# The opening of a two-block network in fp32: identity first, x in two transfers, and two modulation units multiplied without a split

## The chip, the cores and the metric

The kernel runs on one core of a Trainium2 chip. Its time is the device time of one launch in microseconds; the median of the runs is compared. The core has five engines that run instruction streams of their own and meet at semaphores: TensorE (PE, with its weight loads PEld), VectorE (DVE), ScalarE (ACT), GpSimd (POOL) and SyncE (SP), which here only sends transfers.

## What is computed

Two transformer blocks on 256 tokens of width 1024, everything in fp32. Only the beginning of the first block matters here:

```python
mod = jax.nn.silu(c) @ w_ada[l] + b_ada[l]          # c: 1024 numbers, w_ada: 1024 x 6144
sh1, sc1, gt1, sh2, sc2, gt2 = jnp.split(mod[:, None, :], 6, axis=-1)
mod_c = jax.nn.silu(c_ctx) @ w_ada[l] + b_ada[l]
h = modulate(rmsnorm(x, g_norm1[l]), sh1, sc1)      # x: 256 x 1024
hc = modulate(rmsnorm(ctx, g_norm1[l]), shc1, scc1) # ctx: 256 x 1024
cq, ckv, kpe, rq, rk, rv, rg = split_proj(h @ w_in[l])
cq_c, ckv_c, kpe_c, rq_c, rk_c, rv_c, rg_c = split_proj(hc @ w_in[l])
```

The first 2048 columns of mod hold the shift sh1 and the scale sc1, without which no h can be made. What follows (two kinds of attention, retention, feed-forward networks, the second block) is the same before and after.

## The kernel before

All weights stream through six raw buffers of 128 x 1024 numbers. A "unit" is one such load, mostly 512 KB: two row tiles of 128 by 512 columns. Units are numbered in the order in which they are used. u0 to u15 are the modulation (panels ada0 to ada3, four units each, of 512 columns), u16 is the first half of cq, u17 and u18 the first two units of rq, u19 the second half of cq, u20 and u21 the rest of rq, u22 to u25 ckvpe (the latent keys), then rk and so on.

TensorE multiplies in the fast format fp32r, so each unit is split: ScalarE copies the raw unit to `w_hi` (rounded), VectorE subtracts it from the raw one into `w_lo`. There are three pairs of split buffers (NSPLIT = 3). VectorE's subtraction raises `unit_ready` by one; TensorE waits for it, and so does SP before it loads the raw buffer again, six units later. The helper `feed_units(n)` on ScalarE and VectorE issues the splits of all units below n that it has not issued yet; where these calls stand among the other work is an order written out by hand, and it decides what waits behind what.

A modulation unit is four products of 512 columns: `c_parts` holds the high and the low halves of silu(c) and silu(c_ctx) in the stationary side, and each of two row tiles is multiplied by `w_hi` and by `w_lo`. `ada(p)` on ScalarE copies the finished row of 512 numbers of a panel into `modrow`; `ada_spread(p)` on TensorE turns it into columns; `spread(p)` on VectorE adds the bias; `gain_column` makes the gain of the norm. x is normalised (`square`, `variance`, GpSimd's power, `scale_rows` on VectorE for the first 128 tokens and `scale_row` on ScalarE for the others) and turned by TensorE in pairs of column tiles (`turn("x1", ...)`); each pair is then made full with gain and shift (`full`, by VectorE or ScalarE) and written as a high and a low half. cq needs pairs 0 and 1 for its first unit and 2 and 3 for its second; rq's units need pair 0, 1, 2 and 3 in turn.

`keep_busy(o, n)` issues n transposes of the identity that nobody reads; BUSY says how many stand where. `chunk_unit` is a modulation unit followed by three of them. `turn_vectors(g)` turns the small vectors of group g (0: c and c_ctx; 1: gains, biases; 2 and 3: the convolution's) into columns, which VectorE copies in `columns(g)`. `claim` takes a PSUM bank and waits until its last user has freed it; `next_small` goes round the banks 4 to 7, and ckvpe claims all four of them before its first product.

The start: SP sends u0, u1, u2, all of x, u3, u4, u5, then the fourteen vectors of groups 1 to 3, then u6 and so on, each from then on when the unit six before is released. ctx follows u15. The norm's tables k1, the decays and the gains follow u19. ScalarE's own queue sends c, c_ctx and the first block of constants `k0` (identity, selector, ones) before its first instruction.

## Time and profile before

| | us |
|---|---|
| median of 3 runs | 863.7 (862.12 to 865.11) |
| the profiled execution | 862.75 |
| its span, first to last instruction | 860.9 |
| TensorE busy | 833.5 (97%) |
| VectorE busy | 588.4 (68%) |
| ScalarE busy | 469.7 (55%) |
| TensorE idle in the first 60 us | 60 - 47.35 = 12.65 |

Durations come from the profiled execution. A busy TensorE is modelled: the record of a product reaches over the start of the next one, so the cost of a product is read from start to start. L901 and the like are lines of the kernel; names such as raw, w_hi or bank stand without their buffer numbers. `k` as an operand is the identity's block.

### The profile page before, as it was taken

The page shows a single profiled execution, that of the slowest core. Times are in us where ns is not written, and L with a number is a line of the kernel's source. Part 1 is how long each engine was busy: PE and PEld are TensorE (multiplying, and loading weights), DVE is VectorE, ACT ScalarE, POOL GpSimd, SP SyncE. Part 2 cuts the span into 40 slices and gives each one's busy share as a digit, 9 for nine tenths or more (in the row PEclk, how much of TensorE's full clock was granted, in tenths as well). Part 3 has the DMA queues.
Part 4 walks back from the last instruction along what each step waited for, and adds up shares of the span by engine and source line. Part 5 has one row for each costly group of instructions (what it writes and reads, how often), then busy time and mean ns, then how long its engine had stood idle before and what let it go on. Part 6 is the DMA issues. An engine that isn't in the chain of part 4 may idle for free. (4 is left out here: it accounts for less than half of the span.)

```text
span 860.9 us, 12797 instructions
## 1 busy us (share of the span) xinstructions
PE 833.5 (97%) x4917; PEld 719.5 (84%) x4917; DVE 588.4 (68%) x917; ACT 469.7 (55%) x757; POOL 17.8 (2%) x24
## 2 busy tenths in 40 slices
PE   5999999999999999999999999999999999999997
PEld 4788888867899999997889977788977788888785
DVE  4775968797687778887756777577446655555444
ACT  6686355266456666663546584556535644454442
POOL 1001000000000000000000000010000000000000
PEclk9999999999999999999999999999999999999999
DMA  9964464154656655568648543244505565555541
GB/s 329 356 221 125 147 209 147 49 160 161 203 180 210 188 177 183 176 204 310 237 148 295 183 152 123 74 138 156 195 4 170 171 195 178 189 179 189 185 157 49
DMA packets 103507, 152.85 MB, mean 178 GB/s; under 512 B 6506, under 2 KB 55702, under 8 KB 103448
## 3 DMA queue, kind: packets, MB, share of 16 engines
q1 hardware_dynamic: 102136, 149.15, 52.9%
q10 hardware_dynamic: 1312, 2.90, 0.9%
q8 instruction: 39, 0.64, 0.3%
q14 instruction: 20, 0.16, 0.1%
HBM read 150.97 MB, written 1.05 MB: 177 GB/s over the span
## 5 line engine op out<-in xcount | busy, mean ns | idle before, releaser
L2071 DVE TENSOR_TENSOR w_lo<-raw,w_hi 128x1024 fp32r<-128x1024 f32 (+1 forms) x244 | 294.5, 1213 | 163.7 <-ACT w_hi L1510 163.0
L1510 ACT ACTIVATE w_hi<-raw 128x1024 fp32r<-128x1024 f32 (+1 forms) x244 | 254.7, 1050 | 205.1 <-PE bank L737 141.7
L735 PE MATMUL bank<-w_hi,hT_hi 128*128 128x512 f32 (+2 forms) x400 | 156.1, 390 | 2.9 <-DVE w_lo L2071 2.4
L737 PE MATMUL bank<-w_hi,hT_lo 128*128 128x512 f32 (+2 forms) x400 | 153.0, 382 | 0.0
L736 PE MATMUL bank<-w_lo,hT_hi 128*128 128x512 f32 (+2 forms) x400 | 152.7, 382 | 0.0
L839 PE MATMUL bank<-hT_hi,w_hi 128*128 128x256 f32 x512 | 145.1, 283 | 0.0
L840 PE MATMUL bank<-hT_lo,w_hi 128*128 128x256 f32 x512 | 145.0, 283 | 0.0
L841 PE MATMUL bank<-hT_hi,w_lo 128*128 128x256 f32 x512 | 145.0, 283 | 0.0
L839 PEld LDWEIGHTS bank<-hT_hi,w_hi 128*128 128x128 f32 x512 | 98.3, 192 | 0.0
L840 PEld LDWEIGHTS bank<-hT_lo,w_hi 128*128 128x128 f32 x512 | 98.3, 192 | 0.0
L841 PEld LDWEIGHTS bank<-hT_hi,w_lo 128*128 128x128 f32 x512 | 98.3, 192 | 0.0
L735 PEld LDWEIGHTS bank<-w_hi,hT_hi 128*128 128x128 f32 x400 | 75.2, 188 | 19.1 <-DVE w_lo L2071 2.8
L737 PEld LDWEIGHTS bank<-w_hi,hT_lo 128*128 128x128 f32 x400 | 75.2, 188 | 14.8
L736 PEld LDWEIGHTS bank<-w_lo,hT_hi 128*128 128x128 f32 x400 | 75.3, 188 | 13.2
L735 PE MATMUL bank<-w_hi,act_hi 128*128 128x512 f32 x176 | 70.7, 402 | 0.3 <-DVE w_lo L2071 0.3
L737 PE MATMUL bank<-w_hi,act_lo 128*128 128x512 f32 x176 | 69.6, 396 | 0.0
L736 PE MATMUL bank<-w_lo,act_hi 128*128 128x512 f32 x176 | 69.6, 395 | 0.0
L735 PEld LDWEIGHTS bank<-w_hi,act_hi 128*128 128x128 f32 x176 | 33.1, 188 | 9.5 <-issue 1.6
L736 PEld LDWEIGHTS bank<-w_lo,act_hi 128*128 128x128 f32 x176 | 33.1, 188 | 8.1 <-issue 0.5
L737 PEld LDWEIGHTS bank<-w_hi,act_lo 128*128 128x128 f32 x176 | 33.1, 188 | 8.0
L1478 POOL TENSOR_TENSOR rstd<-var,mhalf 128x2 f32<-128x2 f32 (+3 forms) x18 | 15.8, 876 | 838.7 <-DVE var L2728 256.2
L1130 PEld LDWEIGHTS bank<-k,prob 128*128 128x128 f32 x104 | 12.3, 141 | 15.5 <-issue 6.8
(341 smaller groups left out, 1197.5 us busy)
## 6 DMA issues: line engine op xcount, KB each, us to landing
raw<-w_up_dram SPq DMA_DIRECT2D x132, 256.0 KB, 3.1
raw<-w_ada_dram SPq DMA_DIRECT2D x48, 512.0 KB, 4.7
raw<-w_down_dram SPq DMA_DIRECT2D x44, 512.0 KB, 3.4
raw<-w_in_dram SPq DMA_DIRECT2D x40, 512.0 KB, 4.3
raw<-w_gate_dram SPq DMA_DIRECT2D x44, 256.0 KB, 2.8
raw<-w_out_dram SPq DMA_DIRECT2D x16, 512.0 KB, 3.3
raw<-wk_x_dram SPq DMA_DIRECT2D x8, 512.0 KB, 4.5
raw<-wv_x_dram SPq DMA_DIRECT2D x8, 512.0 KB, 3.3
```

The lines of the kernel that those rows point to most:

```text
L735: pe.matmul(o, xh, yh, start=first, stop=False, skip_group_check=skip)
L736: pe.matmul(o, xh, yl, start=False, stop=False, skip_group_check=skip)
L737: return pe.matmul(o, xl, yh, start=False, stop=last, skip_group_check=skip)
L839: pe.matmul(o, hi[:, c:c + P], xh[:, k, :], start=f, stop=False, skip_group_check=True)
L840: pe.matmul(o, hi[:, c:c + P], xl[:, k, :], start=False, stop=False, skip_group_check=True)
L841: ins = pe.matmul(o, lo[:, c:c + P], xh[:, k, :], start=False, stop=last, skip_group_check=True)
L1130: ins = pe.transpose(o[:, j * P:(j + 1) * P], prob_of(i)[:, j * P:(j + 1) * P], ident)
L1478: pool.tensor_tensor(rstd[:, r, c:w], var[:, r, c:w], mhalf[:, c:w], ALU.pow).then_inc(rstd_ready, 1)
L1510: act.activation(unit_view(w_hi[n % NSPLIT], u), unit_view(raw[u % NRAW], u), ACT.Copy).then_inc(w_hi_ready, 1)
L2071: dve.tensor_tensor(unit_view(w_lo[n % NSPLIT], u), unit_view(raw[u % NRAW], u), unit_view(w_hi[n % NSPLIT], u).bitcast(F32), ALU.subtract ...
```

## The change

The identity alone goes first on SP's queue, and the selector and the ones go on ScalarE's. x is sent in two halves, behind u4 and u6, each with a semaphore of its own. The convolution's vectors go behind u19, ctx goes behind u17. ScalarE does one Silu on a scratch column before anything else, and does not split any unit before c_parts is made; VectorE likewise. Twelve filler transposes stand ahead of the first product, while those behind u6 to u10 are gone. Units u14 and u15 are multiplied as they landed, in plain fp32, two products a unit in place of four; nobody splits them, and a tiny copy on VectorE raises `unit_ready` by two for them when TensorE is done. `ready_at` gives the new order of these counts. The spreads and the turns of x move among the units, and the fourth spread goes behind cq's first unit. The convolution's vectors are turned behind rq, and their columns and the lower bound's arithmetic are done behind ctx.

```diff
--- before.py
+++ after.py
@@ -272,7 +272,7 @@
-BUSY = {"score": 8, "ada": 3, "cq": 8, "ffnpre": 14, "gu0": 8}
+BUSY = {"score": 8, "start": 12, "ada": 3, "cq": 8, "ffnpre": 14, "gu0": 8}
 BY_ROW_TILE = ("wout2_1", "wo1", "dn1")
@@ -310,10 +310,20 @@
-    split_units = [u for u in range(len(units)) if not summed[u]]
+    direct = (first_unit["ada3"] + 2, last_unit["ada3"])
+    split_units = [u for u in range(len(units)) if not summed[u] and u not in direct]
     split_of = {u: n for n, u in enumerate(split_units)}
...
     inner = np.cumsum([u not in ends and not summed[u] for u in range(len(units))]).tolist()
+
+    given = [u for u in range(first_unit["rq"] + 1) if u not in direct] + list(direct)
+    given += range(first_unit["rq"] + 1, len(units))
+    ready_at = {u: n + 1 for n, u in enumerate(given)}
+
+    landed, landings = {}, [0] * NRAW
+    for u, (_, _, _, _, sources) in enumerate(units):
+        landings[u % NRAW] += 16 * len(sources)
+        landed[u] = landings[u % NRAW]
@@ -506,11 +516,12 @@
         in_ident = sem("in_ident")
+        in_sel = sem("in_sel")
         in_k1 = sem("in_k1")
...
         in_ctxx = sem("in_ctxx")
-        in_x = sem("in_x")
+        in_x = [sem(f"in_x{t}") for t in range(T)]
         in_gate = sem("in_gate")
@@ -701,8 +712,6 @@
-        landed = {}
-
         block = ctx.enter_context(nc.Block())
@@ -775,14 +784,18 @@
                             before(k)
-                    pe.wait_ge(unit_ready, u + 1)
-                    hi, lo = halves_of_unit(u, nk)
+                    if u in direct:
+                        pe.wait_ge(raw_landed[u % NRAW], landed[u])
+                        hi, lo = unit_view(raw[u % NRAW], u).rearrange("p (k n) -> p k n", k=nk), None
+                    else:
+                        pe.wait_ge(unit_ready, ready_at[u])
+                        hi, lo = halves_of_unit(u, nk)
                     final = u == last_unit[name]
...
                             k = first_k + kk
-                            ins = step(k, use, hi[:, kk, :], lo[:, kk, :], begin and kk == 0, final and kk == nk - 1)
+                            ins = step(k, use, hi[:, kk, :], None if lo is None else lo[:, kk, :], begin and kk == 0, final and kk == nk - 1)
                         if final:
@@ -907,6 +920,8 @@
                 def step(k, use, hi, lo, first, last):
+                    if lo is None:
+                        return pe.matmul(ps(use)[:, :], c_parts[:, k, :].bitcast(F32), hi, start=first, stop=last)
                     pe.matmul(ps(use)[:, :], c_parts[:, k, :], hi, start=first, stop=False)
@@ -938,48 +953,54 @@
-            pe.wait_ge(c_lo_ready, 2)
             for p in range(4):
                 claim((f"ada{p}", 0), p)
+            keep_busy(ps(("ada3", 0))[:, 0:P], BUSY["start"])
+            pe.wait_ge(c_lo_ready, 2)
...
-            for p in range(2):
-                chunk = ada_steps(p)
-                for _ in range(4):
-                    chunk_unit(chunk)
-                run(chunk)
-                if p == 0:
-                    for g in range(1, len(VEC_GROUPS)):
-                        turn_vectors(g)
+            chunk = ada_steps(0)
+            for _ in range(4):
+                chunk_unit(chunk)
+            run(chunk)
+            chunk = ada_steps(1)
+            chunk_unit(chunk)
+            chunk_unit(chunk)
+            turn_vectors(1)
+            next(chunk)
+            pe.wait_ge(in_sel, 16)
             ada_spread(0, 0)
+            run(chunk)
             chunk = ada_steps(2)
-            chunk_unit(chunk)
+            next(chunk)
+            next(chunk)
+            ada_spread(1, 1)
+            next(chunk)
             turn("x1", None, range(2))
-            chunk_unit(chunk)
-            ada_spread(1, 1)
-            chunk_unit(chunk)
-            turn("x1", None, range(2, 4))
             run(chunk)
...
             next(chunk)
+            turn("x1", None, range(2, 4))
             ada_spread(2, 2)
             run(chunk)
-            ada_spread(3, 3)
...
             next(cq)
+            ada_spread(3, 7)
             next(rq)
...
             run(rq)
+            for g in range(2, len(VEC_GROUPS)):
+                turn_vectors(g)
             rows_panel("ckvpe", hT_hi, hT_lo, turn_before("ctx"), cT, b=4)
@@ -1427,26 +1448,26 @@
         def _(sp):
-            count = [0] * NRAW
+            sp.dma_start(ident, const[:, C_ID:C_ID + P]).then_inc(in_ident, 16)
             for u, (name, k0, nk, cols, sources) in enumerate(units):
...
-                    sp.wait_ge(unit_ready, u - NRAW + 1)
+                    sp.wait_ge(unit_ready, ready_at[u - NRAW])
                 dst = unit_view(raw[slot], u).rearrange("p (k n) -> p k n", k=nk)
...
                     sp.dma_start(dst[:, :, c0:c0 + width], src).then_inc(raw_landed[slot], 16)
-                    count[slot] += 16
-                landed[u] = count[slot]
-                if u == NRAW - 1:
-                    for group, done in ((1, in_vec), (2, in_conv), (3, in_conv)):
+                for group, done, at_unit in ((1, in_vec, NRAW - 1), (2, in_conv, first_unit["rq"] + 2),
+                                             (3, in_conv, first_unit["rq"] + 2)):
+                    if u == at_unit:
                         for name, _ in VEC_GROUPS[group]:
...
                             sp.dma_start(vrow[g][r:r + n, :], vec_src[name]).then_inc(done, 16)
-                if u == 2:
-                    sp.dma_start(res[:, :, :], a["x"].rearrange("(t p) d -> p t d", p=P)).then_inc(in_x, 16)
-                if u == last_unit["ada3"]:
+                for t in range(T):
+                    if u == (4, 6)[t]:
+                        sp.dma_start(res[:, t, :], a["x"][t * P:(t + 1) * P, :]).then_inc(in_x[t], 16)
+                if u == first_unit["rq"]:
                     sp.dma_start(in_ctx[:, :, :], a["ctx"].rearrange("(t p) d -> p t d", p=P)).then_inc(in_ctxx, 16)
@@ -1501,7 +1522,7 @@
                     fed[0] += 1
-                    if summed[u]:
+                    if summed[u] or u in direct:
                         continue
@@ -1521,7 +1542,9 @@
                 act.dma_start(vrow[g][r:r + n, :], vec_src[name]).then_inc(in_c, 16)
-            act.dma_start(k0[:, :], const[:, 0:C_RCOS]).then_inc(in_ident, 16)
+            act.dma_start(k0[:, C_SEL:C_RCOS], const[:, C_SEL:C_RCOS]).then_inc(in_sel, 16)
+            act.wait_ge(mhalf_ready, 1)
+            act.activation(expsink[:, 0:1], mhalf[:, 0:1], ACT.Silu)
@@ -1585,7 +1608,6 @@
-            feed_units(2)
             emptied(act, ("vec", 0))
@@ -1604,21 +1626,22 @@
-            feed_units(4)
-            act.wait_ge(in_x, 16)
+            feed_units(6)
+            act.wait_ge(in_x[0], 16)
             square("x1", 0, 0, res[:, 0, :])
-            feed_units(6)
-            square("x1", 0, 1, res[:, 1, :])
-            feed_units(7)
             ada(0)
             feed_units(8)
+            act.wait_ge(in_x[1], 16)
+            square("x1", 0, 1, res[:, 1, :])
+            feed_units(10)
             scale_row("x1", res[:, 1, :], row[:, 1, :])
...
             ada(2)
+            feed_units(16)
+            full("x1", 1)
             feed_units(first_unit["cq"] + 1)
-            full("x1", 1)
             ada(3)
@@ -2061,6 +2084,8 @@
                         continue
+                    if u in direct:
+                        continue
                     if units[u][0].startswith("down") and u + 1 < len(units) and summed[u + 1]:
@@ -2159,7 +2184,6 @@
-            feed_units(1)
             columns(0)
@@ -2188,21 +2212,15 @@
             feed_units(6)
+            columns(1)
+            feed_units(8)
             variance("x1")
-            for g in range(1, len(VEC_GROUPS)):
-                columns(g)
+            feed_units(9)
+            scale_rows("x1", [res[:, 0, :]], [row[:, 0, :]])
+            feed_units(10)
             emptied(dve, ("vec", 1))
-            lb = vec("hgrn_lb_2")
-            step(dve.tensor_tensor(lbc[:, 0, :], lb[:, 0:HH], lb[:, HH:2 * HH], ALU.max))
-            settle()
-            for i in range(2):
-                dve.tensor_tensor(lbc[:, 1 + i, :], lb[:, i * HH:(i + 1) * HH], lbc[:, 0, :],
-                                  ALU.subtract).then_inc(lb_in_ready, 1)
-            feed_units(7)
-            scale_rows("x1", [res[:, 0, :]], [row[:, 0, :]])
-            feed_units(11)
             spread(0)
-            feed_units(13)
+            feed_units(12)
             spread(1)
@@ -2211,6 +2229,9 @@
             spread(3)
+            dve.wait_ge(w_used, inner[direct[0]])
+            ready(dve, ("end", "ada3"))
+            dve.tensor_copy(sums[:, 0:1], csilu[:, 0, 0:1]).then_inc(unit_ready, len(direct))
             gain_column(0, modc[:, 8:16], "g_norm1", [("spread", 1), ("spread", 3)], slice(KD // 2, KD))
@@ -2222,6 +2243,14 @@
             turn("ctx", None, range(2, 4))
+            for g in range(2, len(VEC_GROUPS)):
+                columns(g)
+            lb = vec("hgrn_lb_2")
+            step(dve.tensor_tensor(lbc[:, 0, :], lb[:, 0:HH], lb[:, HH:2 * HH], ALU.max))
+            settle()
+            for i in range(2):
+                dve.tensor_tensor(lbc[:, 1 + i, :], lb[:, i * HH:(i + 1) * HH], lbc[:, 0, :],
+                                  ALU.subtract).then_inc(lb_in_ready, 1)
```

## Rows read from the trace of the kernel before

**Rows 1.** Busy time by window of all engines, with its line of columns; us from the start.

```profile
core 0: us, PE busy (x) PEld busy (x) DVE busy (x) ACT busy (x) POOL busy (x), PEclk, DMA share, GB/s
...
4.00:14.00 10.00, 3.76 (x11) 2.97 (x12) 4.59 (x7) 6.67 (x10) 0.00 (x0) 1.00 1.05 394
...
60.00:120.00 60.00, 60.00 (x312) 51.54 (x311) 47.76 (x98) 26.84 (x60) 2.83 (x4) 1.00 0.53 174
```

**Rows 2.** Timeline of the start: start us, us, engine, line, operation, out<-in, count [idle<-releaser].

```profile
6.80 0.28 PE L901 MATMUL bank<-k,vrow 16*128 16x16 f32 x1 [6.80 <-DMA k<-shape_constants_dram]
...
7.25 1.28 ACT L1590 ACT_TABLE_LOAD   x1
...
8.88 0.72 ACT L1594 ACTIVATE c_parts<-csilu 128x256 fp32r<-128x256 f32 x2
...
10.52 0.80 PE L910 MATMUL bank<-w_hi,c_parts 128*128 128x512 f32 x1 [3.44 <-DVE c_parts L2167]
```

**Rows 3.** Packets of ScalarE's queue from 3.5 to 4.5 us: packets, MB, share.

```profile
q10 hardware_dynamic: 16, 0.00, 2.9%
```

**Rows 4.** Timeline of SP: issues of units u5 and u7 (columns of rows 2).

```profile
3.98 0.54 SPq L1439 DMA_DIRECT2D raw<-w_ada_dram  x1
...
11.63 0.39 SPq L1439 DMA_DIRECT2D raw<-w_ada_dram  x1
```

**Rows 5.** The same two issues, u5 then u7: count, KB, us to landing.

```profile
raw<-w_ada_dram SPq DMA_DIRECT2D x1, 512.0 KB, 10.6
...
raw<-w_ada_dram SPq DMA_DIRECT2D x1, 512.0 KB, 7.4
```

**Rows 6.** Timeline, 17 to 32 us: square, scaled row, low halves, spread, turned pairs.

```profile
17.60 1.04 ACT L1532 ACTIVATE junk<-res 128x1024 f32<-128x1024 f32 x1
...
20.91 0.74 DVE L2102 TENSOR_SCALAR row<-res,rstd 128x1024 f32<-128x1024 f32 x1
...
23.13 3.50 DVE L2071 TENSOR_TENSOR w_lo<-raw,w_hi 128x1024 fp32r<-128x1024 f32 x3 [0.34 <-ACT w_hi L1510]
...
24.20 0.95 PE L938 MATMUL bank<-k,modrow 128*128 128x2 f32 x8
...
30.65 1.04 PE L878 MATMUL bank<-k,row 128*128 128x128 f32 x8
```

**Rows 7.** Timeline of TensorE: modulation products, then one fp32 score product.

```profile
14.31 0.63 PE L911 MATMUL bank<-w_lo,c_parts 128*128 128x512 f32 x1
...
15.68 0.40 PE L911 MATMUL bank<-w_lo,c_parts 128*128 128x512 f32 x1
...
15.91 0.40 PE L910 MATMUL bank<-w_hi,c_parts 128*128 128x512 f32 x1
...
189.48 1.08 PE L1109 MATMUL bank<-kT,qT 96*128 96x512 f32 x2
...
190.39 0.60 PE L1130 MATMUL bank<-k,prob 128*128 128x128 f32 x4
```

**Rows 8.** Timeline, 36 to 48 us: u16's high half, copy, cq0, fourth spread, rq0, rq1.

```profile
36.88 1.06 ACT L1510 ACTIVATE w_hi<-raw 128x1024 fp32r<-128x1024 f32 x1 [1.72 <-DMA raw<-w_in_dram]
...
38.74 0.59 ACT L1605 ACTIVATE modrow<-bank 128x512 f32<-128x512 f32 x1
...
41.28 0.36 PE L735 MATMUL bank<-w_hi,hT_hi 128*128 128x256 f32 x1
...
42.49 0.15 DVE L2177 TENSOR_TENSOR modc<-bank,vcol 128x4 f32<-128x4 f32 x1
...
44.23 0.40 PE L735 MATMUL bank<-w_hi,hT_hi 128*128 128x512 f32 x1
...
47.55 0.50 PE L735 MATMUL bank<-w_hi,hT_hi 128*128 128x512 f32 x1 [0.42 <-DVE w_lo L2071]
```

**Rows 9.** Timeline, 59 to 61 us: last low halves of ctx, first product of ckvpe.

```profile
59.52 1.29 DVE L2132 TENSOR_TENSOR hcT_lo<-fbuf,hcT_hi 128x512 fp32r<-128x512 f32 x2 [0.70 <-ACT hcT_hi L1555]
...
60.52 0.29 PE L735 MATMUL bank<-w_hi,hT_hi 128*128 128x288 f32 x1
```


## Prediction

> **What bounds the kernel now.** I read three views, in this order. First the busy time by window: from 60 us on TensorE is busy in every microsecond of the stretch shown, while in the opening the 16 DMA engines are the ones with no idle time, moving 394 GB/s from 4 to 14 us [rows 1]. So nothing that is saved in the opening is of use unless it moves the moment from which TensorE runs without a gap; and once that moment has moved, the whole rest moves with it. That is why the sum below is a list of times at a few places, before and after, and not a sum of busy times. Then the timeline of the first 62 us, from gate to gate. The reader is to see these gates. TensorE's first work waits for the identity until 6.80, its first product for the halves of c until 10.52 [rows 2]. Then come sixteen modulation units (u0 to u15), then cq0 (u16) at 41.28, then rq0 (u17), then rq1 (u18), which waits for its low half until 47.55 [rows 8]; from there TensorE has no gap until ckvpe starts at 60.52 [rows 9]. Last, each transfer's issue and time to landing [rows 4, 5]: a unit of 512 KB takes 0.524 MB / 394 GB/s = 1.33 us of the queues.
>
> **The first product.** The identity goes first on SP's queue, so it lands before the rows of c and c_ctx, whose 16 packets move between 3.5 and 4.5 us [rows 3]. The transpose that stood at 6.80 can therefore start at about 4.3 (bounds 4.0 and 4.8). From it to the first product there were 10.52 - 6.80 = 3.72 us, in which 1.28 was the second table load, before Silu. The change does Silu once on a scratch column while the engine has nothing else to do, and I take the copies to run under the same table, as they did after 8.53. But two splits that stood before that chain now stand behind it. c_parts began 2.08 after the transpose, so now 0.80 after it, at 5.1; its two copies end at 5.85; the high half of u0 takes 1.06 [rows 8] and the low half about 1.2 (three in 3.50 [rows 6]). First product at 8.1 instead of 10.52: 2.4 us earlier. The twelve filler transposes run from 4.6 to about 7.1 and keep nobody waiting.
>
> The Trainium skill (ScalarE: Activation LUTs, What ACT_TABLE_LOAD costs) puts a switch of table at about 2.66 us with its drain. The trace shows 7.25 + 1.28 = 8.53 and c_parts at 8.88 after two small Silus, so here it is 1.28; by the page the first product would come 1.4 us earlier still, and the sum would not change, since the next gate hides it.
>
> **Units 6 to 9: the gate moves to the transfers.** SP's order is now u0 to u4, half of x, u5, ten short vectors, u6, the other half of x, u7. Up to u7 the bytes are those of before less the four vectors of the convolution. Before, u5 landed at 3.98 + 10.6 = 14.6 and u7 at 11.63 + 7.4 = 19.0 [rows 4, 5]: 4.4 us for two units that need 2.7, so the fourteen vectors took about 1.7. By rows of 512 bytes (176 of 284) the four take 1.1 of it, by transfers (4 of 14) 0.5. So u7 lands between 17.9 and 18.5, and I take 18.2; a launch with every penalty as before gives 19.0, one with none of the vectors' time 17.3. SP is not late for it: it can send u6 only when u0 is released, near 8.1, and by then has about issued the vectors. Behind u7's landing stands a chain of both vector engines in the new order: high half of u7 1.06; square of the second half of x 1.04 + 0.19; high half of u8 1.06; low half of u8 1.17; scaled row 0.74 (GpSimd's power is done by then); low half of u9 1.17 [rows 6, 8]. That is 6.4, so u9 is multiplied at 24.6. Even with an early landing u9 would not come before 22.7: VectorE copies the vectors' columns only after TensorE has turned them behind u5 (about 16.8), and then does u6 to u9 and the row, 4 x 1.2 + 0.74.
>
> The Trainium skill (DMA: Bandwidth & Descriptors, Bandwidth) wants transfers of at least 1 MiB for 75% of the peak, which speaks against x in two halves. The window from 4 to 14 us moves mostly 512 KB transfers at 394 GB/s with the engines full [rows 1], so here the split costs no bandwidth; by the page u7 would land up to a third of a transfer, 0.9 us, later, and the end with it.
>
> **Units 9 to 15: TensorE itself.** From u9 on every split is ready in time, so the stretch is what TensorE issues. Warm products of 512 columns start 15.91 - 15.68 = 0.23 apart [rows 7], 0.94 a unit. Then: u9 to u13, five units, 4.7; two spreads 2 x 0.9; two pairs of x turned, 2 x 0.87 (recorded 0.95 and 1.04 long, the tails over the next operation taken off [rows 6]). The last two units are plain fp32: no such product with c_parts is in the trace, but its like is. A score product of the first attention is fp32 with 512 columns; it is recorded twice, and from its start at 189.48 to the next operation at 190.39 it takes 0.91 [rows 7]. Bounds: 0.47, if it went as two passes, and 1.08, if its records had to end before the next could start. Four of them are 3.64 where eight fp32r products were 1.88: +1.8 on TensorE, for which ScalarE sheds 2 x 1.06 and VectorE 2 x 1.2 that TensorE waited on little. Total 4.7 + 1.8 + 1.7 + 3.6 = 11.8, so the last modulation product ends its issue at 36.4. From its end to cq0 the chain is the copy of the row (0.6), two high halves, the last low half: 41.28 - 38.74 = 2.5 [rows 8]. Before, that copy stood behind the landing of u16, which came at 36.88 because ctx was ahead of it; with ctx moved behind u17 this is no gate (u16 lands near 31). cq0 starts at 36.6 + 2.5 = 39.1, 2.2 us earlier than at 41.28.
>
> **What takes it back.** (1) The fourth spread now stands behind cq0's 24 products, which take 44.23 - 41.28 = 2.95 [rows 8]. It starts at 42.1, ends at 43.1; VectorE reads it at 43.15, where before it read it at 42.49. From that reading to rq1 there were 47.55 - 42.49 = 5.06: gain column, two pairs made full, high halves, the split of u18, which ScalarE holds behind all of those. VectorE's new tiny copy, which releases u14 and u15, adds 0.1. rq1 at 48.3, against 47.55: +0.75. What waits behind the wait of that copy is this same chain, and SP, which can send u20 only then, near 43.4; it lands near 48 and its split is wanted at 55, so that costs nothing. rq0, which could start at 43, is done at 45.9, so TensorE stands about 2.4 us idle before rq1; here the 2.2 us vanish. (2) The convolution's vectors are now turned after rq in the small banks 7 and 4. ckvpe claims all of banks 4 to 7 before its first product, so it waits until VectorE has copied both, and VectorE comes to that only behind the last low half of ctx, which ended at 59.52 + 1.29 = 60.81, while ckvpe began at 60.52 [rows 9]. Two copies of some 0.2, the handover 0.1: ckvpe at 61.35 on the old clock, +0.8. The bounds are 0.25 (the transposes alone, if the copies came early) and 1.0.
> The other moves (ctx later, constants in two parts, lower-bound arithmetic behind ctx, other fillers) have their users at least 2 us behind: ctx lands near 34 and is squared near 48.
>
> **Sum.** +0.75 + 0.8 = +1.5 us; my start times carry about 0.2 of rounding, so I take +1.4. The profiled execution lasted 862.75 with a span of 860.9, that is 0.95 under the median of the runs, 863.7; the difference is put on the median: 865.1, written 865.0. The bounds of the parts: u7 at 17.3 instead of 18.2, -0.9; its landing at 19.0, +0.8; fp32 at 0.47 or 1.08, -1.8 or +0.7; the second take-back -0.5 or +0.2. Not all fall on one side: 862 to 867.
>
> **Rivals.** (A) *The gain is kept.* If the chain behind the fourth spread were not what rq1 waits for (say ScalarE's full pair and VectorE's overlap more than before), rq1 would start when rq0 is done, at 45.9, 1.65 early; with the early u9 at 22.7 and without the bank wait, cq0 is at 37.2 and rq1 at 44.0: -3.5, or 860.2. For it: 2.4 us of TensorE's idle time lie there. Against it: the code has the same order in that chain as before, when it took 5.06. Chance 0.12, of which most is under 861.1.
> (B) *The clock.* The change takes away the fillers behind u6 to u10. Before, the record of a product is 0.63 us long at 14.31 and 0.40 at 15.91, which fits 1.2 and 2.4 GHz, 4.7 us after TensorE began to work without gaps at 10.52 [rows 2, 7]; the granted clock of the window reads 1.00 all the same [rows 1]. In the new order TensorE is busy in less than half of the time between 16.7 and 24.6. If its clock falls there and needs 4.7 us of work to rise again, the stretch from 24.6, which is TensorE's own, loses half of that: +2.3, so 867.4. The point from which it decides is a fall after u6; a slow clock before u6 is hidden by u7's landing. For it: the thin fillers; against it: from 38 to 40 us in the old run the engine was idle most of the time and the products after it were fast at once (24 products in 2.95 [rows 8]). Chance 0.2, and it is the slow side by itself.
> (C) *Nothing changes:* the gates shift, both take-backs are half as large, 863.7. This is part of the forecast's range. Chance 0.18.
> (D) The forecast, 864 to 866.3: 0.5.
>
> **Chances.** A measurement of this kernel can tell about 0.3%, 2.6 us, from no change: under 861.1 is faster, over 866.3 slower. Faster gets 0.12 from A; slower 0.22, all of B and the forecast's upper tail; the rest, 0.66, is the same. The range that leaves out 2 in 10 reaches into both sides: 861.5 to 868.5.
>
> **What would show it.** First product near 8.1; u7's landing near 18.2 and u9 multiplied near 24.6; the four fp32 products 0.91 apart; cq0 near 39.1; a gap of TensorE of 2 us and more before rq1 (L735), released by VectorE's low half; ckvpe behind VectorE's copy of the vectors' columns; from there on the old trace, shifted by about 1.4. Wrong would be: rq1 before 46.5, fp32 products under 0.6, records of 0.6 us for 512 columns after 20 us, or a difference that arises after 75 us, of which nothing here speaks.

## The result, and the profile after

Against runs of the kernel before on the same chip, the changed kernel takes 865.57 us (median of 20, 864.07 to 868.34), the kernel before 863.02 (median of 20, 861.66 to 865.81). The ratio is 1.0031, 95% interval 1.0023 to 1.0039: slower by 2.7 us by the ratio (2.55 by the medians), at the edge of the 0.3% that the prediction took as what can be told from no change. It forecast 865.0, in a range of 861.5 to 868.5. That the median lies only 0.6 us from the forecast is in part luck: the prediction counted +1.4 us from a median of before of 863.7, which in this comparison is 863.02.

The profiled execution lasted 866.0 us with a span of 864.1, against 862.75 and 860.9 before. First the page's head:

```profile
span 864.1 us, 12793 instructions
...
PE 836.8 (97%) x4914; PEld 721.4 (83%) x4914; DVE 586.6 (68%) x916; ACT 467.0 (54%) x755; POOL 17.8 (2%) x24
```

Then the busy time by window of the changed kernel, with the line of its columns; the last row answers to [rows 1].

```profile
core 0: us, PE busy (x) PEld busy (x) DVE busy (x) ACT busy (x) POOL busy (x), PEclk, DMA share, GB/s
...
16.00:20.40 4.40, 2.63 (x12) 2.04 (x13) 2.67 (x4) 3.58 (x6) 0.00 (x0) 1.00 1.05 391
20.40:28.00 7.60, 7.60 (x29) 6.42 (x27) 5.86 (x9) 6.35 (x7) 0.70 (x1) 0.55 1.04 376
28.00:38.00 10.00, 10.00 (x51) 7.24 (x51) 5.20 (x10) 3.82 (x6) 0.00 (x0) 1.00 1.00 333
...
64.00:120.00 56.00, 56.00 (x294) 48.21 (x293) 44.58 (x94) 24.62 (x54) 2.83 (x4) 1.00 0.49 154
```

From 64 us on it is the old picture: TensorE without a gap. The loss is made before that. And one row is new: from 20.4 to 28.0 us the granted clock is 0.55 of full speed, that is 1.2 GHz for nearly all of it, where the kernel before had 1.00 throughout the opening.

The gates, from the timeline of the changed kernel (columns as in [rows 2]); they answer to [rows 2], [rows 7], [rows 8] and [rows 9]:

```profile
4.26 0.25 PE L914 MATMUL bank<-k,vrow 16*128 16x16 f32 x1 [4.26 <-DMA vrow<-c_ctx_dram]
...
8.17 0.47 PE L925 MATMUL bank<-w_hi,c_parts 128*128 128x512 f32 x1 [0.91 <-DVE w_lo L2096]
...
17.93 0.27 DVE L2185 COPY vcol<-bank 128x108 f32<-128x108 f32 x1 [1.71 <-PE bank L914]
...
18.25 1.06 ACT L1531 ACTIVATE w_hi<-raw 128x1024 fp32r<-128x1024 f32 x1 [0.82 <-DMA raw<-w_ada_dram]
...
19.39 0.50 PE L925 MATMUL bank<-w_hi,c_parts 128*128 128x512 f32 x1 [1.49 <-DVE w_lo L2096]
...
23.85 0.63 PE L926 MATMUL bank<-w_lo,c_parts 128*128 128x512 f32 x1
24.28 0.63 PE L925 MATMUL bank<-w_hi,c_parts 128*128 128x512 f32 x1
...
34.49 3.60 PE L924 MATMUL bank<-raw,c_parts 128*128 128x512 f32 x8
...
37.92 1.04 PE L756 MATMUL bank<-k 128*128 128x128 f32 x8
...
40.66 0.35 PE L744 MATMUL bank<-w_hi,hT_hi 128*128 128x256 f32 x1 [1.71 <-DVE hT_lo L2157]
...
44.60 0.16 DVE L2201 TENSOR_TENSOR modc<-bank,vcol 128x4 f32<-128x4 f32 x1 [2.64 <-PE bank L953]
...
49.66 0.50 PE L744 MATMUL bank<-w_hi,hT_hi 128*128 128x512 f32 x1 [2.27 <-DVE w_lo L2096]
...
62.89 0.41 DVE L2185 COPY vcol<-bank 128x88 f32<-128x88 f32 x2
...
63.53 0.37 PE L744 MATMUL bank<-w_hi,hT_hi 128*128 128x288 f32 x1 [0.60 <-DVE vcol L2185]
```

The opening is quicker where the change meant it to be: the first product starts at 8.17 instead of 10.52. cq0 comes at 40.66 instead of 41.28, so 0.62 of the 2.35 us is left. Then rq1 comes at 49.66 instead of 47.55, and ckvpe at 63.53 instead of 60.52: what was a gain of 0.62 is a loss of 3.01, and most of it is in the two waits in brackets, 2.27 for a low half (0.42 before) and 0.60 for the vectors' copy. The waits of TensorE up to 70 us (what it waited for: us in total, times, longest) have nothing else after cq0:

```profile
PE bank L925 <- DVE w_lo L2096: 3.7, 3, 1.5
PE bank L744 <- DVE w_lo L2096: 2.3, 1, 2.3
PE bank L744 <- DVE hT_lo L2157: 1.7, 1, 1.7
PE bank L744 <- DVE vcol L2185: 0.6, 1, 0.6
```

### The profile page after: what moved, and what is told of

It reads as the page before. It is cut to its first block and busy times, and to the rows that moved or that the text cites. A ratio compares the mean times of both kernels' runs of the same rounds, so it can differ in the third digit from the quotient of the medians.

```text
span 864.1 us, 12793 instructions
## 1 busy us (share of the span) xinstructions
PE 836.8 (97%) x4914; PEld 721.4 (83%) x4914; DVE 586.6 (68%) x916; ACT 467.0 (54%) x755; POOL 17.8 (2%) x24
## 5 line engine op out<-in xcount | busy, mean ns | idle before, releaser
L2096 DVE TENSOR_TENSOR w_lo<-raw,w_hi 128x1024 fp32r<-128x1024 f32 (+2 forms) x242 | 292.2, 1212 | 157.3 <-ACT w_hi L1531 156.0
L1531 ACT ACTIVATE w_hi<-raw 128x1024 fp32r<-128x1024 f32 (+2 forms) x242 | 252.7, 1050 | 202.9 <-PE bank L746 142.4
```

The source lines that it names most:

```text
L1531: act.activation(unit_view(w_hi[n % NSPLIT], u), unit_view(raw[u % NRAW], u), ACT.Copy).then_inc(w_hi_ready, 1)
L2096: dve.tensor_tensor(unit_view(w_lo[n % NSPLIT], u), unit_view(raw[u % NRAW], u), unit_view(w_hi[n % NSPLIT], u).bitcast(F32), ALU.subtract ...
```

## The experiments

My theory: two places take back more than the start gives (the fourth spread behind cq0; the vectors' copies ahead of ckvpe), and the fall of the clock adds to it in part of the runs. The rivals: the new start is itself of no use or harm; the missing fillers or the fp32 products carry the loss. Each kernel was run 5 to 12 times. Each ratio is to the kernel before in the same session, whose medians were 862.65 (the first four), 862.33 (the next four) and 862.57 (the last four).

**One part undone: the fourth spread** (from the changed kernel).

```diff
-            next(cq)
             ada_spread(3, 7)
+            next(cq)
```

> The changed kernel with one edit: the fourth spread goes back ahead of cq's first unit. Theory G (gates): in the changed kernel rq1 waited 2.27 us for its low half, because VectorE could read the fourth spread only at 44.60, behind cq0. Ahead of cq0 the spread (0.95 us) fits into the 1.71 us that TensorE waits there anyway, so cq0 stays at about 40.7, VectorE reads it right behind the low half of u17, near 41.9, and rq1 starts near 47.0 instead of 49.66: 2.3 to 2.7 us less in the whole, the wait before rq1 under 0.6 us. Theory C (the clock alone costs the time): rq1's wait is only moved, and the kernel gets faster by less than 0.7 us.

Measured: 861.83 us, ratio 0.9988 (0.9977 to 0.9998), where the changed kernel had 1.0031: 3.7 us better, 2.7 by the lowest times. TensorE, VectorE and TensorE again in its timeline:

```profile
39.51 0.36 PE L744 MATMUL bank<-w_hi,hT_hi 128*128 128x256 f32 x1
...
40.72 0.15 DVE L2201 TENSOR_TENSOR modc<-bank,vcol 128x4 f32<-128x4 f32 x1
...
45.78 0.50 PE L744 MATMUL bank<-w_hi,hT_hi 128*128 128x512 f32 x1 [0.42 <-DVE w_lo L2096]
...
59.66 0.37 PE L744 MATMUL bank<-w_hi,hT_hi 128*128 128x288 f32 x1 [0.57 <-DVE vcol L2185]
```

The chain is the same in both; only its start moved, from 3.94 us after cq0's first product (44.60 - 40.66) to 1.21 after it, and rq1 stands 6.27 behind cq0 again, as in [rows 8], instead of 9.00. That is 2.73 us, the time by which the lowest runs differ. The rest of the 3.7 fits the clock (this profile has no fall, and none of the 12 runs has a granted clock of 0.995 or less, where six of the changed kernel's 20 do), but why fewer runs fall is not shown. The wait for the vectors' copy is still there, 0.57.

**One part undone: the place of the vectors' columns.** turn_vectors(2) and (3) go between rq1 and cq1, and VectorE's two copies (columns(2) and (3)) behind variance("ctx").

```diff
             next(rq)
             next(rq)
+            for g in range(2, len(VEC_GROUPS)):
+                turn_vectors(g)
             run(cq)
             turn("ctx")
             run(rq)
-            for g in range(2, len(VEC_GROUPS)):
-                turn_vectors(g)
```

> The changed kernel with one edit: the convolution's vectors are turned between rq1 and the second unit of cq, and VectorE copies them before the first half of ctx is scaled, so that banks 7 and 4 are free long before ckvpe claims them. Theory G: ckvpe starts right behind rq's last product, 0.9 us earlier than now against that product (63.53 - 62.61), of which 0.2 is the transposes that are only moved: 0.6 to 0.8 us less in the whole. Rival (ckvpe waits for the last low half of ctx in any case): its start moves by less than 0.3 us and the time does not change.

Measured: 865.01 us, 1.0020 (1.0006 to 1.0033); by the lowest times 0.67 better than the changed kernel, as expected, though by the ratios the two intervals overlap. No wait stands ahead of ckvpe any more. The distance from rq1 to ckvpe can't be read in this profile, because its products are 0.43 apart from 49.7 to 52 us. It can be read where the spread is undone too: 13.88 in the profile above, 13.12 in the one with two parts undone below, 0.76 less. Up to rq1 this program is that of the changed kernel, and its profile shows it at full clock:

```profile
38.87 0.36 PE L744 MATMUL bank<-w_hi,hT_hi 128*128 128x256 f32 x1 [1.71 <-DVE hT_lo L2157]
...
47.86 0.50 PE L744 MATMUL bank<-w_hi,hT_hi 128*128 128x512 f32 x1 [2.26 <-DVE w_lo L2096]
```

**The fillers back** behind u6 to u10, at five places of the changed kernel, and the reverse, **the kernel before without its fillers** there. The diff is of one place of the first; the second has it the other way round.

```diff
-            next(chunk)
+            chunk_unit(chunk)
```

> The changed kernel with one edit: three filler transposes again behind each of u6 to u10. Theory C: the products of 512 columns stay 0.23 us apart throughout, where the changed kernel's profile had them 0.43 apart from 20.4 to 28.0; the granted clock of the span is 0.998 or more in every run where it was 0.994 in a third of them; runs of the slow kind (span near 864 and 866) vanish and the median falls by 1 to 2 us to the level of the other runs, 864.3. The fillers themselves cost up to 0.36 us each where TensorE is the bound (u9, u10), so the runs with a full clock get slower by 0.3 to 0.7. Rival (the clock falls whatever the fillers): same share of runs with 0.994, and 0.5 us slower.

> The kernel before with one edit: the fillers behind u6 to u10 taken away. Theory C: the clock falls in some of the runs after 17 us as it does in the changed kernel: products 0.43 apart for some us, a granted clock of 0.994 to 0.996 in those runs, and these 1.5 to 2 us longer than the rest; median 0 to 1.5 us above the kernel before. Rival (the fall belongs to the new order of transfers and the early start): full clock in every run, and 0 to 0.5 us faster than the kernel before.

Measured: with fillers 866.03 us, 1.0034 (1.0025 to 1.0044); its lowest run is 1.2 above the changed kernel's lowest, so the fillers cost more than I expected (0.3 to 0.7). Its runs' granted clocks are 0.996 to 1.00, where six of the changed kernel's 20 had 0.994 or 0.995. The worst falls are gone, but seven of the 12 runs are at 0.996 or 0.997, where I had expected 0.998 in every run, and the median did not fall by the expected 1 to 2 us: the fillers cost about as much as they give. The kernel before without them: 863.26 us, 0.9999 (0.9985 to 1.0012). Eleven of its 12 runs have a mean clock of 0.997 or less (11 of the 35 runs of the kernel before beside them do), and the one at 0.999 took 860.6, 1.0 below the lowest of the kernel before. Its profile shows the slow clock further on, from about 40 us:

```profile
38.00:50.00 12.00, 9.79 (x50) 9.44 (x51) 8.44 (x14) 9.06 (x14) 0.00 (x0) 0.72 0.77 275
```

So taking the fillers out is about neutral in either kernel: about 1 us better in the fastest runs, as much worse where the clock falls.

**One part undone: the two direct units** split again, in the changed kernel (VectorE's small copy that released them goes too).

```diff
-    direct = (first_unit["ada3"] + 2, last_unit["ada3"])
+    direct = ()
```

> The changed kernel with one edit: u14 and u15 are split into halves and multiplied in fp32r again (and VectorE's copy that released them is gone). Theory G: TensorE is the bound from u9 to u15, and the four fp32 products took 37.92 - 34.49 = 3.43 us there where eight fp32r products take 1.88; ScalarE and VectorE were idle for 2.58 and 2.02 us around that time, so the splits come for nothing. cq0 starts 1.5 us earlier and everything behind it too: 1.2 to 1.6 us less in the whole. Rival (the direct units pay for themselves, because the splits of u14 and u15 would hold up u16's and the pairs of x): no change, or slower.

Measured: 864.5 us, 1.0024 (1.0014 to 1.0033): 0.6 us better by the ratios, 0.85 by the lowest times, less than the 1.2 to 1.6 expected. The profiled execution lost more to the clock than that of the changed kernel did; the same window as above:

```profile
20.40:28.00 7.60, 7.60 (x24) 6.25 (x24) 5.34 (x9) 5.63 (x7) 0.71 (x1) 0.50 1.02 374
```

It is the one part whose price a single undoing doesn't give cleanly, so I measured it again from a quieter kernel. **All three undone** (spread first, columns early, units split), and **two undone**, the direct units kept. The edits are the diffs above, three of them and two.

> The changed kernel with three edits together: the fourth spread ahead of cq0, the convolution's vectors turned before cq's second unit, and u14 and u15 split again. Theory G: the three add up, 2.7 + 0.7 + up to 1.5, since they stand one behind the other on the same path, but rq1's wait for the split of u18 can then come from the transfers (ctx is ahead of u18). About 4 to 4.9 us under the changed kernel in runs with a full clock, that is 1.5 to 2.5 us under the kernel before, a ratio to it of 0.997 to 0.998. Rival (one gate stands right behind another, so the gains overlap): no better than the first edit alone, 0.9988.

> The changed kernel with the fourth spread ahead of cq0 and the convolution's vectors turned early, but u14 and u15 multiplied as landed in fp32. Against the kernel of the three undone edits (0.9971) this is the price of the two direct units where nothing else stands behind them: theory G says 1.5 us, so 0.9987 to 0.9990 to the kernel before. Rival (the direct units pay in part for themselves): under 0.8 us, 0.9980 or less.

Measured: three undone 859.68 us, 0.9971 (0.9962 to 0.9980); by the lowest times 4.9 better than the changed kernel, as expected of the sum. Two undone 860.91 us, 0.9979 (0.9970 to 0.9988). Their timelines of TensorE (u9, the direct products where there are any, cq0), three undone first:

```profile
25.01 0.50 PE L925 MATMUL bank<-w_hi,c_parts 128*128 128x512 f32 x1 [0.91 <-DVE w_lo L2096]
...
38.06 0.36 PE L744 MATMUL bank<-w_hi,hT_hi 128*128 128x256 f32 x1
```

```profile
24.70 0.50 PE L925 MATMUL bank<-w_hi,c_parts 128*128 128x512 f32 x1 [0.61 <-DVE w_lo L2096]
...
32.99 3.60 PE L924 MATMUL bank<-raw,c_parts 128*128 128x512 f32 x8
...
39.16 0.36 PE L744 MATMUL bank<-w_hi,hT_hi 128*128 128x256 f32 x1
```

From u9 to cq0 it is 13.05 without and 14.46 with the direct units: 1.4 us. The times say 0.7 (ratios, two sessions) to 1.5 (lowest times). By the ratio the expectation was missed: 0.9979 lies where I had put the rival, 0.9980 or less. That the units cost is shown; whether 0.7 or 1.4 is not settled.

**One part alone: the new start in the kernel before** (identity first, selectors apart, Silu once ahead, splits behind the vectors' columns, 12 fillers).

```diff
+            sp.dma_start(ident, const[:, C_ID:C_ID + P]).then_inc(in_ident, 16)
-            act.dma_start(k0[:, :], const[:, 0:C_RCOS]).then_inc(in_ident, 16)
+            act.dma_start(k0[:, C_SEL:C_RCOS], const[:, C_SEL:C_RCOS]).then_inc(in_sel, 16)
+            act.wait_ge(mhalf_ready, 1)
+            act.activation(expsink[:, 0:1], mhalf[:, 0:1], ACT.Silu)
-            feed_units(2)
```

> The kernel before with the start of the changed one alone: identity first on SP's queue, selector and ones on ScalarE's, the Silu on a scratch column, no split ahead of c_parts, twelve fillers; x in one transfer, the vectors and ctx where they were, all units split. Theory G: first product near 8.2 instead of 10.52, but the landings of u6 to u8 and then that of u16 behind ctx (36.85) stand where they stood, so that cq0 starts at 41 as before: 0 to 0.6 us faster. Rival (the path runs through TensorE's first product): 2 us or more faster.

Measured: 861.76 us, 0.9996 (0.9987 to 1.0004): a start that is 2.3 us earlier is worth nothing that can be told (0.4 us by the ratio). Its first product is at 8.21, and at each gate behind it less is left: u6 starts 1.0 us earlier than before (20.05, was 21.04), cq0 0.9 (40.41, was 41.28), and the span is 0.6 shorter (860.3). The first take is at u3, for whose landing behind x ScalarE waits 2.86; another gate is u16, whose landing stands behind ctx in this kernel as in the old one (there 36.88, [rows 8]):

```profile
12.01 1.06 ACT L1514 ACTIVATE w_hi<-raw 128x1024 fp32r<-128x1024 f32 x1 [2.86 <-DMA raw<-w_ada_dram]
...
35.10 1.06 ACT L1514 ACTIVATE w_hi<-raw 128x1024 fp32r<-128x1024 f32 x1 [0.97 <-DMA raw<-w_in_dram]
```

**Is u7's landing the gate of u6 to u9?** The prediction said so. Only 128 of the 1024 columns of x's second half are loaded, the rest is set to zero by GpSimd, so u7 can land 0.459 MB / 394 GB/s = 1.2 us earlier. The change, in the loop that loads x:

```diff
-                        sp.dma_start(res[:, t, :], a["x"][t * P:(t + 1) * P, :]).then_inc(in_x[t], 16)
+                        sp.dma_start(res[:, t, 0:(D, 128)[t]], a["x"][t * P:(t + 1) * P, 0:(D, 128)[t]]).then_inc(in_x[t], 16)
```

> The changed kernel with most of one transfer left out: of the second half of x only 128 of 1024 columns are loaded, and the rest is filled with zeros on GpSimd at the start, so its output is another one; all work on the engines is the same. That is 0.46 MB, 1.15 us of the queues, less ahead of u7. Theory G (u7's landing is the gate of the stretch from u6 to u9): u7 lands near 17.1 instead of 18.25, u8 and u9 and all behind them come about 1.1 us earlier; TensorE's wait of 1.5 us before u7's neighbour shrinks and the whole gets 0.8 to 1.2 us shorter in runs of the same clock. Rival (that stretch is bound by VectorE's and ScalarE's order of work): less than 0.4 us.

Measured: 865.79 us, 1.0038 (1.0024 to 1.0053). Nothing gained. In the profiled execution the landing was not what decided; its timeline shows what did:

```profile
19.55 0.27 DVE L2187 COPY vcol<-bank 128x108 f32<-128x108 f32 x1 [1.84 <-PE bank L914]
...
21.01 0.50 PE L925 MATMUL bank<-w_hi,c_parts 128*128 128x512 f32 x1 [1.49 <-DVE w_lo L2098]
...
23.89 0.76 DVE L2129 TENSOR_SCALAR row<-res,rstd 128x1024 f32<-128x1024 f32 x1 [0.60 <-POOL rstd L1500]
```

VectorE stands idle for 1.84 us until TensorE has finished u5 and turned the vectors, copies them, and only then makes the low half of u6, for which TensorE waits 1.49. Each engine waits for the other once, and both waits are in the changed kernel too (1.71 and 1.49, above). Further on, the scaled row waits 0.60 for GpSimd's power. But this execution is one whose products are 0.43 apart until 14 us, so that u5 ends late. In the changed kernel's own profile, quick from the start, VectorE waits for the high half of u8, which ScalarE makes only behind u7's landing at 18.25:

```profile
21.33 1.23 DVE L2096 TENSOR_TENSOR w_lo<-raw,w_hi 128x1024 fp32r<-128x1024 f32 x1 [0.69 <-ACT w_hi L1531]
...
23.14 1.22 DVE L2096 TENSOR_TENSOR w_lo<-raw,w_hi 128x1024 fp32r<-128x1024 f32 x1
```

The second is the low half of u9. Which of the two chains ends last there differs between the nine profiles that copy the vectors early and send x in two parts. Where VectorE's copy came by 18.22 (the changed kernel, vectors early, units split again, two undone) the landing's chain is last; where it came at 18.62 or later (spread first, fillers back, three undone, short x, no start fillers) it is the round trip with the power behind it. The times of this profile are not to be laid beside the others' directly: its first transpose is at 5.07, theirs at 4.2 to 4.8.

**The round trip taken away**, from the kernel with three parts undone; then the same with the short x; then without the 12 fillers of the start.

```diff
             feed_units(6)
-            columns(1)
             feed_units(8)
             variance("x1")
             feed_units(9)
             scale_rows("x1", [res[:, 0, :]], [row[:, 0, :]])
             feed_units(10)
+            columns(1)
```

The third one's edit is in BUSY:

```diff
-"start": 12
+"start": 0
```

> The kernel of the three undone edits (ratio 0.9971 to before) with one more: VectorE copies the columns of vector group 1 only behind the low half of u9, where the first bias is wanted, in place of ahead of the low half of u6. Theory D (the stretch from u6 to u9 is gated by the round trip TensorE, VectorE, TensorE behind u5: VectorE stood 1.8 us idle until TensorE had turned those vectors): the low half of u6 is done 1.5 us or more before TensorE wants it, u6 follows u5 at once, and the whole gets 0.8 to 1.5 us shorter, ratio 0.9955 to 0.9962. Theory G as the prediction had it (u7's landing is the gate): u6 moves but u9 does not, under 0.4 us, ratio 0.9967 to 0.9975.

> The same kernel as the one with the late columns, and again only 128 of 1024 columns of the second half of x are loaded, the rest zeros, so its output is another one and the work of the engines is the same. Theory D: once the round trip is gone, the transfers are the next gate, so that here the missing 1.15 us of the queues shows: another 0.5 to 1.1 us shorter than with the late columns alone. If it is TensorE at half clock or its own work that is next, the two are the same within 0.3 us.

> The kernel of the three undone edits without the twelve filler transposes ahead of the first product. In three profiles of the new start the first products were 0.43 us apart until 13 to 15 us and in one they were 0.23 apart from 8.2 on, all with the fillers. Theory C: without them TensorE is idle from 4.5 to 8.1, its products are 0.43 apart until 12.9 or later in every run, the loss is hidden by the transfers and the round trip in part: 0 to 0.8 us slower than 0.9971, 1.5 at the most. Rival (the fillers are of no use, since the pause behind them undoes them): the same within 0.3 us.

Measured: columns late 859.23 us, 0.9956 (0.9943 to 0.9968), better than both kernels of this case. With the short x 858.35, 0.9948 (0.9936 to 0.9961): 0.85 us under it by the lowest times, in the same session. The timeline of columns late, ScalarE and TensorE:

```profile
18.07 1.06 ACT L1531 ACTIVATE w_hi<-raw 128x1024 fp32r<-128x1024 f32 x1 [0.94 <-DMA raw<-w_ada_dram]
...
18.45 0.50 PE L925 MATMUL bank<-w_hi,c_parts 128*128 128x512 f32 x1 [0.85 <-DVE w_lo L2096]
...
37.25 0.36 PE L744 MATMUL bank<-w_hi,hT_hi 128*128 128x256 f32 x1
```

u6 starts 14.23 us after the first transpose (18.45 - 4.22); in the changed kernel it was 15.13 (19.39 - 4.26). Now the landing counts: the same short x that gave nothing in the changed kernel gives 0.85. The short x was not run on the three undone alone, so the pair also differs in the three parts, which stand behind u9. By how much columns late beats three undone stays open: 1.3 us by the ratios (what the round trip's theory expected), 0.45 by the medians and 0.1 by the lowest (what the landing's theory expected), in different sessions.

Without the start's fillers: 859.83 us, 0.9963 (0.9951 to 0.9976), against 0.9971 with them. No use of them can be measured. Its profile begins with slow products, but so do most profiles that have the fillers.

## Why the prediction was right and where it was not

**The first product.** Forecast 4.3 and 8.1, seen 4.26 and 8.17. One table load is left, at 2.10, while ScalarE has nothing else to do. The Trainium skill (ScalarE: Activation LUTs, What ACT_TABLE_LOAD costs) would have put the product 1.4 us earlier; the trace doesn't bear that out.

**u7's landing.** The time was right (18.25 for 18.2). The Trainium skill (DMA: Bandwidth & Descriptors, Bandwidth) gave up to 0.9 us more for x in two halves; u7 landed as if there were no such price, with 391 GB/s moved from 16 to 20.4 us. Its role was right only in part, and this is the step that failed: the prediction put the whole stretch behind the landing (u9 at 24.6) and named VectorE's wait for the turned vectors only as a bound, 22.7, "even with an early landing". In the changed kernel's profile the landing's chain does set the low half of u9, ready at 23.14 + 1.22 = 24.36; TensorE, at half rate, came to u9 only at 25.13. With two undone the same chain gives u9 at 24.70. But with three undone it is the round trip, and it ends as late:

```profile
18.69 0.27 DVE L2185 COPY vcol<-bank 128x108 f32<-128x108 f32 x1 [1.82 <-PE bank L914]
...
23.07 0.75 DVE L2127 TENSOR_SCALAR row<-res,rstd 128x1024 f32<-128x1024 f32 x1 [0.60 <-POOL rstd L1499]
```

From the start of that copy to u9 it is 25.01 - 18.69 = 6.3 us, where the bound had 5.5 (4 x 1.2 + 0.74) from vectors turned at 16.8. Two terms were short. The copy came 0.8 to 2.7 later than 16.8 (17.61 to 19.55 in the nine profiles), because the landing of u5 or slow products held u5 back. And GpSimd's power, "done by then", was put at nothing, where the scaled row waits for it. In such an execution a shorter landing gains nothing; in one like the changed kernel's profile TensorE at half rate comes last. That these two make the whole of the short x's missing gain is argued from the profiles, not shown run by run. Two gates 1 us apart give nearly the same sum, and a right time for u9 is no proof of the reason.

**Units 9 to 15.** The four fp32 products start 37.92 - 34.49 = 3.43 us apart from the next operation, 0.86 each; forecast 0.91, read off the score product [rows 7]. cq0 was forecast for 39.1. At full clock it is 38.87 with the vectors early, where the program up to there is the changed kernel's, and 39.51 and 39.16 in the profiles of the spread and of two undone, where the spread lies in TensorE's wait for the halves. In the changed kernel's own profile it is 40.66, because its products are 0.43 apart until 28: the fall costs about 1.8 us against 38.87, where B had 2.3.

**The two take-backs.** rq1 came 9.00 behind cq0 (forecast 48.3 - 39.1 = 9.2; before 6.27), TensorE idle for 2.27 ahead of it (forecast 2.4), released by VectorE's low half. ckvpe came 13.87 behind rq1, before 12.97: +0.90 for the forecast +0.8. Undoing them one at a time gave back 2.7 and 0.67 by the lowest times. Rival A, that the gain is kept, needed rq1 before 46.5; it did not happen here, and came about (45.78) once the spread was undone.

**The sum.** Both take-backs stand in the forecast at +1.5. The 14 runs of the changed kernel at a granted clock of 0.997 and more have a median of 864.8, 1.75 above the median of before, and the lowest runs are 2.4 apart: the shift without the falls is somewhat more than forecast, by how much is not settled. The rest is rival B, whose mechanism came true, but not in all runs: the clock falls after u6, and TensorE's own stretch from there is run at half rate. Six of the 20 runs, at 0.994 or 0.995, took 865.9 to 868.3, and they lift the median by 0.8, to 865.57. So the shift is +2.55 to +2.7, between the forecast's +1.4 and B's +3.7. I treated the fall as a case that happens or not; it is one that happens in a part of the executions, and belongs into the sum with that part.

**Fillers and direct units.** The prediction priced the removed fillers at nothing save for B. That is right at the level of the sum: they cost about what they save. For the direct units it had +1.8 on TensorE; the three comparisons give 0.6 to 1.5, so this term was too large, though its fp32 products were nearly as long as forecast (0.86 for 0.91).

## What to carry to other kernels

Work that is saved ahead of a chain of gates pays only if each gate behind it moves too: list the gates' times and follow the saving through them, as the new start alone shows, with 2.3 us won at the first product and at most 0.6 at the end. When a small step is moved behind a block of a pipelined engine, price the whole chain that hangs on it, not the step: the spread of 1 us cost 2.7. And where two gates lie within 1 us, take one away and then the other before you name the cause, and look in more than one execution which of them ended last.

## What the hardware showed that I had not expected

With one and the same new start there are two kinds of profiles. In three (the changed kernel, units split again, columns late) the products behind 8.1 us are 0.23 apart at once, as at 2.4 GHz. In the other nine they are 0.43 apart until 11.5 to 15 us, among them the one whose start has no fillers. Its first product:

```profile
8.16 0.76 PE L925 MATMUL bank<-w_hi,c_parts 128*128 128x512 f32 x1 [3.66 <-DVE w_lo L2096]
```

against 0.47 in the changed kernel. In both kinds with fillers TensorE then waits 0.91 us for the first low half.

The three that were fast at once are just the three that fell to half rate between 17 and 28 us, when TensorE had waited twice; here the last of them, busy by window (columns as above):

```profile
20.40:24.20 3.80, 3.61 (x9) 2.12 (x8) 3.12 (x5) 3.80 (x5) 0.70 (x1) 0.55 1.05 387
```

None of the nine fell there; two of them did later (near 39 and 49.5 us), as did the kernel before without its fillers (near 40), each behind a pause at cq0 or ahead of rq1. And the granted clock is 1.00 in the record of the slow starts although the products are 0.43 apart, while it is 0.50 to 0.55 in the falls between 17 and 28 us: read the distance between products beside it. Why an execution starts in one way or the other stays open; the kernels with the same start show both.
